# The mLSTM's gate rows computed in nineteen small steps, spread over the attention's heads 0 to 5, in place of nine steps in heads 5 and 6

## The reference, cut to what matters

```python
q_a, k_a, v_a, qk_m, v_m, o_m, gates = jnp.split(proj, splits, axis=-1)
y_attn = axial_gqa_attention(q_a, k_a, v_a, q_norm_g[l], k_norm_g[l], tables)
y_mem = bidirectional_mlstm(qk_m, v_m, o_m, gates, conv_w[l], conv_b[l], gate_b[l], mlstm_norm_g[l])
...
b = jnp.cumsum(fc, axis=-1)                       # fc: log_sigmoid of the forget gate
m_t = jnp.maximum(m_inter, jnp.max(d, axis=-1))   # the running maximum that keeps exp small
w_inter = jnp.exp(m_inter - m_t)
p = jnp.exp(d - m_t[..., None])
```

## Time and profile before

| what | value |
|---|---|
| median of 3 runs | 2306.11 us (2304.2 to 2311.93) |
| the profiled execution | 2316.08 us, its span 2313.9 us |
| mean granted TensorE clock | 0.956 |
| PE busy | 2098.8 us, 91% of the span |
| DVE busy | 1103.0 us, 48% |
| ACT busy | 881.5 us, 38% |
| chain that ended last | PE 76%, DVE 10%, ACT 7% |

### The profile page before, as it was taken

How to read it: one execution, slowest core, us unless ns; L and a number is a source line. 1 busy time by engine, 2 the same in 40 slices (tenths; PEclk the granted TensorE clock), 3 DMA queues, 4 the chain that set the end, 5 groups by cost and what they waited for, 6 DMA issues and landing times.

```text
span 2313.9 us, 23764 instructions
## 1 busy us (share of the span) xinstructions
PE 2098.8 (91%) x9228; PEld 1618.9 (70%) x9228; DVE 1103.0 (48%) x1501; ACT 881.5 (38%) x1330; POOL 57.0 (2%) x111
## 2 busy tenths in 40 slices
PE   3899999979888789999998999997999999998795
PEld 1678866636767478888877888885777876775474
DVE  5686645564654445543344333335333444435544
ACT  3433335544432442222244222225414663445431
POOL 0001000000000000100000000000010000000000
PEclk8999999989989799999999999999999999999897
DMA  7236300100203335633332233333241010002132
GB/s 310 91 119 225 121 10 0 46 0 1 83 1 127 109 114 187 188 105 123 122 118 82 92 99 109 119 118 109 73 132 60 28 37 28 19 6 114 37 136 100
DMA packets 60670, 213.97 MB, mean 92 GB/s; under 512 B 6416, under 2 KB 7568, under 8 KB 60304
## 3 DMA queue, kind: packets, MB, share of 16 engines
q1 hardware_dynamic: 46992, 160.02, 20.7%
q0 software_dynamic: 13568, 52.43, 6.6%
HBM read 184.64 MB, written 25.17 MB: 91 GB/s over the span
## 4 chain that ended last, share of the span: by engine, by line
PE 76%; DVE 10%; ACT 7%; issue 4%; DMA 2%; SPq 1%; DVEq 0%; ACTq 0%
PE ps L869 18%; PE ps L871 18%; PE ps L870 18%; PE ps L1000 8%; PE ps L976 2%; PE ps L977 2%; PE ps L944 2%; ACT w_hi L1213 1%; DMA w_raw<-in_weights 1%; DVE w_lo L1600 1%; ACT x1c L1470 1%; PE ps L959 1%; DVE slot L1596 1%; DMA ada_first<-in_ada 1%; DVE x1c L1596 1%
## 5 line engine op out<-in xcount | busy, mean ns | idle before, releaser
L869 PE MATMUL ps<-h_hi,w_hi 128*128 128x512 f32 x1504 | 612.7, 407 | 76.1 <-DVE w_lo L1600 39.8
L870 PE MATMUL ps<-h_lo,w_hi 128*128 128x512 f32 x1504 | 597.0, 397 | 0.0
L871 PE MATMUL ps<-h_hi,w_lo 128*128 128x512 f32 x1504 | 596.7, 397 | 0.0
L1600 DVE TENSOR_TENSOR w_lo<-w_raw,w_hi 128x1024 fp32r<-128x1024 f32 x216 | 264.5, 1225 | 376.7 <-ACT w_hi L1213 376.6
L869 PEld LDWEIGHTS ps<-h_hi,w_hi 128*128 128x128 f32 x1504 | 289.2, 192 | 154.4 <-DVE w_lo L1600 48.2
L1213 ACT ACTIVATE w_hi<-w_raw 128x1024 fp32r<-128x1024 f32 x216 | 227.2, 1052 | 306.1 <-PE ps L871 231.8
L871 PEld LDWEIGHTS ps<-h_hi,w_lo 128*128 128x128 f32 x1504 | 289.1, 192 | 62.9
L870 PEld LDWEIGHTS ps<-h_lo,w_hi 128*128 128x128 f32 x1504 | 289.8, 193 | 60.3 <-issue 2.9
L1724 DVE TENSOR_REDUCE mh<-ps 128x1 f32<-128x512 f32 x192 | 125.1, 656 | 168.6 <-PE ps L944 91.8
L1000 PE MATMUL ps<-full_pf,full_v 128*128 128x512 f32 x256 | 136.8, 617 | 6.9 <-ACT full_pf L1350 6.9
L869 PE MATMUL ps<-hid_hi,w_hi 128*128 128x512 f32 x352 | 136.9, 389 | 0.0
(11 more groups left out here) (291 smaller groups left out, 2670.4 us busy)
## 6 DMA issues: line engine op xcount, KB each, us to landing
w_raw<-in_weights SPq DMA_DIRECT2D x216, 512.0 KB, 3.5
ada_next<-in_ada POOLq DMA_DIRECT2D x32, 512.0 KB, 5.0
ada_last<-in_ada POOLq DMA_DIRECT2D x24, 512.0 KB, 4.7
ada_first<-in_ada SPq DMA_DIRECT2D x8, 1024.0 KB, 20.9
m_scratch<-y POOLq DMA_DIRECT2D x12, 512.0 KB, 3.0
xt<-in_x SPq DMA_DIRECT2D x2, 2048.0 KB, 11.7
y<-m_scratch SPq DMA_DIRECT2D x4, 1024.0 KB, 6.0
x_again<-in_x SPq DMA_DIRECT2D x8, 512.0 KB, 3.5
```

Of the source, the lines that this page charges most:

```text
L869: e.matmul(o, w_hi[slot][:, tile_of(kw)], hi, start=start, stop=False)
L870: e.matmul(o, w_hi[slot][:, tile_of(kw)], lo, start=False, stop=False)
L871: return e.matmul(o, w_lo[slot][:, tile_of(kw)], hi, start=False, stop=stop)
L1600: return e.tensor_tensor(dst, src, hi.bitcast(F32), ALU.subtract)
```

## The change

The same instructions with the same operand sizes are issued at other places of the list. Parts 0 to 15 of the gates stand at every fourth unit, (0,0,3), (0,0,7), (0,1,3) and so on to (3,1,7); parts 16 to 18, which write where the projection's input lies or need the selector, stand at (5,0,2), (5,0,6) and (5,1,2). The rows move out of 0 to 32 KB into five places that are free in heads 0 to 4, and several share one place (`b_cum` and `n_max` lie in `f_log`, `a_gate` in `i_pre`, `m_max` in `zeros`). So parts 0 to 15 no longer wait for the last projection, and the reload of the first keys and queries from DRAM (`back` on SP) waits for two column copies (`g_cols` at 2).

```diff
@@ -354,7 +354,10 @@
     hook(2, 0, 6, ("klo", "full", 1))
     hook(3, 0, 2, ("vprep", "full", 1))
     hook(5, 0, 0, ("back", 0))
-    for part, where in enumerate(((5, 0, 1), (5, 0, 4), (5, 0, 7), (5, 1, 2), (5, 1, 4), (5, 1, 6), (6, 0, 0), (6, 0, 2), (6, 0, 4))):
+    for part in range(16):
+        i = 3 + 4 * part
+        hook(i // 16, i // 8 % 2, i % 8, ("gate", part))
+    for part, where in ((16, (5, 0, 2)), (17, (5, 0, 6)), (18, (5, 1, 2))):
         hook(*where, ("gate", part))
     keys, states, decays, scores, queries = m_prepare(0)
     for i, steps in enumerate(keys + states[0] + decays[0] + queries[0] + decays[1] + scores + queries[1] + states[1]):
...
@@ -646,11 +648,15 @@
         small_m = Area(172.5, 174)
         a_cols, kc_cols, n_cols = (small_m(f"{n}_cols", [P, KT, 2, 4], F32) for n in ("a", "kc", "n"))
         dec_cols = small_m("dec_cols", [P, 8, KT], F32)
-        area = Area(0, 64)
-        f_pre, f_log, b_cum, a_gate, m_max, i_pre, zeros, n_max = (
-            area(f"g_{n}", [64, T], F32) for n in ("f_pre", "f_log", "b_cum", "a_gate", "m_max", "i_pre", "zeros", "n_max"))
-        sel_raw = area("g_sel_raw", [P, T], F32)
-        k_coef, q_coef = f_pre, i_pre
+        g_dec = small_m("g_dec", [64, KT], F32)
+        f_pre = Area(84, 88)("g_f_pre", [64, T], F32)
+        f_log = Area(140, 144)("g_f_log", [64, T], F32)
+        i_pre = Area(152, 156)("g_i_pre", [64, T], F32)
+        zeros = Area(168.5, 172.5)("g_zeros", [64, T], F32)
+        q_coef = at("g_q_coef", [64, T], F32, xp_at)
+        b_cum = n_max = f_log
+        a_gate, m_max, k_coef = i_pre, zeros, f_pre
+        sel_raw = Area(32, 36)("g_sel_raw", [P, T], F32)


         m_dram = nc.dram_tensor("m_scratch", (N_IN1, P, T), F32, kind="Internal").ap()
...
@@ -1362,33 +1368,38 @@
             def gate(part):
                 gb = col("gate_b")
                 if part == 0:
-                    e.wait_ge(s["w_mm"], N_IN1)
                     e.wait_ge(s["y_out"], no("y1", GA, 1))
+                    e.wait_ge(s["m_kept"], kept(QM + 5, OM + 1))
                     e.activation(f_pre[:, :], y[64:P, GA, :], ACT.Identity, bias=gb[64:P, :]).then_inc(s["g_act"], 1)
                     e.activation(i_pre[:, :], y[0:64, GA, :], ACT.Identity, bias=gb[0:64, :]).then_inc(s["g_act"], 1)
+                elif part == 1:
                     e.wait_ge(s["g_act"], 1)
                     e.activation(f_log[:, :], f_pre[:, :], ACT.Abs).then_inc(s["g_act"], 1)
                     e.wait_ge(s["g_act"], 3)
                     e.activation(f_log[:, :], f_log[:, :], ACT.Exp, scale=-1.0).then_inc(s["g_act"], 1)
+                elif part == 2:
                     e.wait_ge(s["g_act"], 4)
                     e.activation(f_log[:, :], f_log[:, :], ACT.Ln, bias=col("one")[0:64, :]).then_inc(s["g_act"], 1)
...
+                elif part == 15:
                     e.wait_ge(s["g_vec"], 16)
-                    e.activation(nm_stack[0:64, :], m_max[:, :], ACT.Copy, scale=-1.0).then_inc(s["st_hi"], 1)
                     e.activation(q_coef[:, :], q_coef[:, :], ACT.Exp).then_inc(s["g_act"], 1)
                     e.activation(g_dec[:, :], g_dec[:, :], ACT.Exp).then_inc(s["g_act"], 1)
+                elif part == 16:
+                    e.wait_ge(s["w_mm"], N_IN1)
+                    e.activation(nm_stack[0:64, :], m_max[:, :], ACT.Copy, scale=-1.0).then_inc(s["st_hi"], 1)
                     e.wait_ge(s["g_act"], 6)
                     copy(wi_stack[0:64, :], q_coef[:, :]).then_inc(s["st_hi"], 1)
+                elif part == 17:
                     e.wait_ge(s["sel_in"], 16)
                     copy(sel[:, :, :].rearrange("p a b -> p (a b)"), sel_raw[:, :]).then_inc(s["sel_made"], 1)
...
@@ -1745,55 +1756,60 @@

             both = ((slice(0, 32), slice(None, None, 1)), (slice(32, 64), slice(None, None, -1)))

-            def scan(dst, d0, d1, op0, op1):
-
-                for r, o in both:
-                    e.tensor_tensor_scan(dst[r, o], d0[r, o], d1[r, o], 0.0, op0, op1).then_inc(s["g_vec"], 1)
+            def scan(r, dst, d0, d1, op0, op1):
+
+                rows, order = both[r]
+                e.tensor_tensor_scan(dst[rows, order], d0[rows, order], d1[rows, order], 0.0, op0, op1).then_inc(s["g_vec"], 1)
+
+            def chunks(x):
+                return x.rearrange("p (a b) -> p a b", b=P)
+
+            def spread(x, n):
+                return x.unsqueeze(2).to_broadcast([32, n, P])

             def gate(part):
+                fw, bw = slice(0, 32), slice(32, 64)
                 if part == 0:
-                    e.wait_ge(s["w_mm"], N_IN1)
+                    e.wait_ge(s["qk_rot"], 5)
                     e.memset(zeros[:, :], 0.0).then_inc(s["g_vec"], 1)
-                    e.memset(v1[0][:, :, P:P + 1], 1.0).then_inc(s["sums_one"], 1)
-                elif part == 1:
+                elif part == 3:
                     e.wait_ge(s["g_act"], 5)
                     e.scalar_tensor_tensor(f_log[:, :], f_pre[:, :], 0.0, f_log[:, :], ALU.min, ALU.subtract).then_inc(s["g_vec"], 1)
                     e.wait_ge(s["g_vec"], 2)
-                    scan(b_cum, f_log, zeros, ALU.add, ALU.add)
-                elif part == 2:
+                    scan(0, b_cum, f_log, zeros, ALU.add, ALU.add)
+                elif part == 4:
+                    scan(1, b_cum, f_log, zeros, ALU.add, ALU.add)
+                elif part == 5:
                     e.wait_ge(s["g_vec"], 4)
                     tt(a_gate[:, :], i_pre[:, :], b_cum[:, :], ALU.subtract).then_inc(s["g_vec"], 1)
+                elif part in (6, 7):
                     e.wait_ge(s["g_vec"], 5)
-                    scan(m_max, a_gate, a_gate, ALU.max, ALU.max)
+                    scan(part - 6, m_max, a_gate, a_gate, ALU.max, ALU.max)
+                elif part == 8:
                     e.wait_ge(s["g_vec"], 7)
                     e.scalar_tensor_tensor(n_max[:, :], b_cum[:, :], -1.0, m_max[:, :], ALU.mult, ALU.subtract).then_inc(s["g_vec"], 1)
-                elif part == 3:
-                    def chunks(x):
-                        return x.rearrange("p (a b) -> p a b", b=P)
-
-                    def ends(x):
-                        return x.unsqueeze(2)
-
-                    fw, bw = slice(0, 32), slice(32, 64)
-                    e.wait_ge(s["g_vec"], 7)
-                    for r, first in ((fw, P - 1), (bw, 0)):
-                        e.tensor_tensor(chunks(k_coef[r, :]), chunks(a_gate[r, :]), ends(m_max[r, first:T:P]).to_broadcast([32, KT, P]),
-                                        ALU.subtract).then_inc(s["g_vec"], 1)
+                    tt(chunks(k_coef[fw, :]), chunks(a_gate[fw, :]), spread(m_max[fw, P - 1:T:P], KT), ALU.subtract).then_inc(s["g_vec"], 1)
+                elif part == 9:
+                    tt(chunks(k_coef[bw, :]), chunks(a_gate[bw, :]), spread(m_max[bw, 0:T:P], KT), ALU.subtract).then_inc(s["g_vec"], 1)
                     e.memset(q_coef[:, :], 0.0).then_inc(s["g_vec"], 1)
                     e.memset(g_dec[:, :], 0.0).then_inc(s["g_vec"], 1)
+                elif part in (10, 11):
+                    r, first, to = ((fw, P - 1, slice(P, T)), (bw, P, slice(0, T - P)))[part - 10]
                     e.wait_ge(s["g_vec"], 12)
-                    for r, first, to in ((fw, P - 1, slice(P, T)), (bw, P, slice(0, T - P))):
-                        e.tensor_tensor(chunks(q_coef[r, to]), ends(m_max[r, first:first + 6 * P + 1:P]).to_broadcast([32, KT - 1, P]),
-                                        chunks(m_max[r, to]), ALU.subtract).then_inc(s["g_vec"], 1)
-                    tt(g_dec[fw, 1:7], m_max[fw, P - 1:6 * P:P], m_max[fw, 2 * P - 1:7 * P:P], ALU.subtract).then_inc(s["g_vec"], 1)
-                    tt(g_dec[bw, 1:7], m_max[bw, 2 * P:7 * P + 1:P], m_max[bw, P:6 * P + 1:P], ALU.subtract).then_inc(s["g_vec"], 1)
-                elif part == 8:
+                    tt(chunks(q_coef[r, to]), spread(m_max[r, first:first + 6 * P + 1:P], KT - 1), chunks(m_max[r, to]), ALU.subtract
+                       ).then_inc(s["g_vec"], 1)
+                    if part == 11:
+                        tt(g_dec[fw, 1:7], m_max[fw, P - 1:6 * P:P], m_max[fw, 2 * P - 1:7 * P:P], ALU.subtract).then_inc(s["g_vec"], 1)
+                        tt(g_dec[bw, 1:7], m_max[bw, 2 * P:7 * P + 1:P], m_max[bw, P:6 * P + 1:P], ALU.subtract).then_inc(s["g_vec"], 1)
+                elif part == 17:
                     e.wait_ge(s["st_hi"], 1)
                     e.scalar_tensor_tensor(nm_stack[64:P, :], m_max[:, :], -1.0, nm_stack[0:64, :].bitcast(F32), ALU.mult,
                                            ALU.subtract).then_inc(s["st_lo"], 1)
+                    e.wait_ge(s["w_mm"], N_IN1)
+                    e.memset(v1[0][:, :, P:P + 1], 1.0).then_inc(s["sums_one"], 1)
+                elif part == 18:
                     e.wait_ge(s["st_hi"], 2)
```

(31 more changed lines are left out.)

## The result

The changed kernel takes 2283.52 us (median of 4 runs, 2283.29 to 2287.01) against 2308.36 us of the kernel before beside it (4 runs, 2304.2 to 2311.93): ratio 0.9884, 95% interval 0.9865 to 0.9902, so 22.6 to 31.2 us less at 2308.36. The forecast was 28.4 us less and 2278 us, with a range of 2269 to 2292 us. Its profiled execution took 2283.45 us, span 2281.5 us. The timed runs of the kernel before fall into two groups (beside experiments 1 to 4 five from 2303.39 to 2305.76 us and thirteen from 2312.29 to 2315.95 us), so its median depends on how many of each it holds; the kept profile, 2316.08 us, is of the upper group.

The account below looks back on a forecast made before the run. PE was taken as the bound, losing time to waits and low clock beside the gate steps. 31.0 us removed less 2.6 us new waits gives 28.4 us; 2306.1 - 28.4 = 2277.7, forecast 2278 us, range 2269 to 2292 us.

Parts of the forecast that it names:

- The excess: Jobs (5,0) to (6,0) take 75.68 us against 38.94 us undisturbed: 36.7 us too long, of which 31.0 us can go.
- 1.8 + 0.9 + 1.07 us of the old excess: Remains in jobs (5,0) to (6,0): decay matmuls 1.8, mLSTM key transposes 0.9, wait behind mLSTM key products 1.07 us.
- waits (17.2 us): Jobs (5,0) to (6,0): five PE waits ended by an ACT exponential or DVE maximum queued behind gate work, 17.2 us.
- clock (13.7 us): Jobs (5,0) to (6,0): four windows at clock 0.57 to 0.72, opening at or just after PE waits, lose 13.7 us.
- a wait of 2 us or more: Condition for the clock to fall: a piece holds PE for 2 us or more; 1.60 us left it at 1.00.
- The first rival: Heads 0 to 3 lack slack: each DVE piece holds PE by its length less 0.3 us; 17.0 us back, 2295 us, 9%.
- ScalarE's 0.4 + 0.4 us: Head 0: parts 0 and 1, two ACT passes each, exceed the 1.9 us a unit hides; PE waits 0.4 us each.
- The waits of 0.4 to 0.6 us: Sign expected in the profile after: ACT-ended PE waits of 0.4 to 0.6 us at (0,0,4), (0,1,0) and (5,0,3).
- The transposes: Three groups of eight transposes stay as PE work, now in head 3: 1.9 us.
- Part 16's 0.55 us: Head 5: two ACT passes right after the last job's inverse, backlog not yet gone; new PE wait of 0.55 us.
- part 17's 1.0 us: Job (5,0): a 1.2 us DVE pass between last reduction and `mx`, slack 0.3 us; new PE wait of 1.0 us.
- the slower rival: Heads 0 to 3: waits grow until the clock falls, 3.4 us after each of four scans; 40.5 us, 2316 us, 3%.

Follow-up runs that it names:

- experiment 1: Changed kernel with gate parts back in nine old groups at (5,0,1) to (6,0,4), rows at their new addresses; 2306.08 us, ratio 0.9974.
- experiment 2: Changed kernel with only ScalarE's parts 0 to 2 early in head 0, the rest back in old groups in heads 5 and 6; 2300.62 us, ratio 0.9963.
- experiment 3: Changed kernel with the same sixteen parts and spacing, three units later, at units 6 and 2; 2294.61 us, ratio 0.9924.
- experiment 4: Changed kernel with parts 0 to 11 in the old large groups in heads 0 to 2; 2292.15 us, ratio 0.9915.
- experiment 5: Changed kernel with parts 0 to 15 at every second unit of heads 4 and 5, parts 16 to 18 in (6,0); 2291.45 us, ratio 0.991.

## Why the prediction was right

**The excess and what can go of it.** Jobs (5,0) to (6,0) were forecast at about 14.5, 15 and 15 us and measure 14.26, 15.17 and 15.03 us. What the forecast leaves in these three jobs is 1.8 + 0.9 + 1.07 us of the old excess and 0.55 + 1.0 + 0.2 us of new waits, so 36.7 - 3.8 - 1.75 = 31.2 us less; measured are 75.68 - 44.46 = 31.2 us. The division into waits (17.2 us) and clock (13.7 us) stands: experiment 2 removes one wait and its clock together, and in experiments 3 and 4 the waits and the falls behind them add up to most of what those variants lose. That the clock follows waits was argued in the prediction and is shown by experiments 2 to 4 as far as falls come and go with the waits. The prediction's condition for it, a wait of 2 us or more, is too simple. Its own rows have a wait of 2.89 us at 490.51 us that brought no fall, as this window of before shows:

```profile
486.00:498.00 12.00, 6.10 (x19) 1.00 0.00 1
```

Whether a given wait brings the clock down is not settled by its length; the last section has the same wait with and without a fall.

**What a unit hides.** VectorE's pieces in heads 0 to 3 cost nothing (the jobs of heads 1 and 2 take within 0.01 us of what they took before), also the pair of 3.5 us at (0,1,7). The first rival, every piece at its length less 0.3 us, holds only ahead of `mx`, where experiment 3 finds it to 0.2 us in four cases. ScalarE's 0.4 + 0.4 us were right as lengths of jobs (0,0) and (0,1), 0.44 and 0.43 us more. The waits of 0.4 to 0.6 us that were to show them are not in the list of waits, where job (0,0) has 0.18 us and job (0,1) none.

**Terms that were mis-sized.** The transposes were put at 1.9 us in head 3; jobs (3,0) and (3,1) are longer by 1.60 and 0.85 us, 2.45 us. Part 16's 0.55 us measures 0.3 us (14.26 - 12.98 - 0.99), and part 17's 1.0 us measures 0.99. The net is 31.2 - 0.9 - 2.45 = 27.9 us, as counted from job (0,0) to the landmark, against 28.4 us. That the three jobs came out at exactly the forecast 31.2 us is in part luck: (5,0) was put 0.3 us too long and (5,1) 0.2 us too short. The fall of the clock, 3.4 us in the slower rival and in two expectations, costs 1.7 us where a wait stands alone; the average of before was drawn from windows in which TensorE waited again and again.

**The time itself.** 2283.5 us against 2278 us is partly the base: the three runs shown had a median of 2306.1 us, and beside the later groups the same kernel had 2308.4, 2312.7 and 2311.7 us (see its two groups of runs in the section on the result). The other 3 us or so lie within what executions of one kernel vary here: gains of 24.8 us and 27.7 us were measured for the same changed kernel.

**Not tried.** The old kernel with only its groups cut at their own places in heads 5 and 6, without the new addresses: the rows would then still wait for the last projection, and experiment 5 answers nearly the same.

## What to carry to other kernels

Before placing work on an engine beside the critical one, read two numbers from an undisturbed unit: how long the neighbour idles ahead of its item, and how long after its end the item is wanted. In heads 0 to 3 the sum was 2.8 us for VectorE, and single scans of 2.3 us cost nothing there; at every second unit of heads 4 and 5 the same pieces cost 7.85 us, so several must leave enough units between them to work off the backlog. The same piece is not free one place further on: ask of every consumer in the unit whether it has that slack, and keep clear of the one that has none (here the combination of the maxima). And where waits of the critical engine also lower its clock, a wait can be worth more than its length: in one pair of profiles a pass of 1 us less in a group went with 5.8 us less, and an isolated fall cost 1.7 us in five cases.
